# Multiplying the root of the norm in behind the products, in block 1 of a two-block transformer kernel

## What is computed

```python
def rmsnorm(x, g):
    y = xf * lax.rsqrt(jnp.mean(xf * xf, axis=-1, keepdims=True) + RMS_EPS)
    return (y * g).astype(x.dtype)

for l in range(2):
    h = rmsnorm(x, norm_mix_pre[l])
    a_in, b_x, b_b, b_c, q, k, v, gate_in = split_cols(h @ w_in[l], IN_SPLITS)
    ...                                             # pool, convolution, dilated attention, gates
    x = x + rmsnorm(merged @ w_out[l], norm_mix_post[l])
    h = rmsnorm(x, norm_mem_pre[l])
    x = x + rmsnorm(memory_cross_attention(h, mem_n, w_mq[l], w_mkv[l], w_mo[l]), norm_mem_post[l])
    h = rmsnorm(x, norm_ffn_pre[l])
    u = h @ w_up[l];  ua, ub = u[..., :D_FF], u[..., D_FF:]
    y = (jax.nn.silu(causal_dwconv(ua, conv_ffn_w[l])) * ub) @ w_down[l]
    x = x + rmsnorm(y, norm_ffn_post[l])
```

## Time and profile before

| | |
|---|---|
| median of 3 runs | 3808.35 us (3804.64 to 3812.05) |
| the profiled execution | 3807.09 us, span 3805.3 us |
| TensorE busy | 95% of the span |
| TensorE weight loads | 78% |
| VectorE busy | 53% |
| ScalarE busy | 40% |
| GpSimd busy | 6% |
| mean granted TensorE clock | 0.986 of full speed |

### The profile page before, as it was taken

One profiled execution on the slowest core, in us unless ns is written; L12 is line 12 of the kernel. 1 busy time (PEld: TensorE's weight loads), 2 busy tenths in 40 slices (PEclk: granted clock), 3 DMA queues, 4 the chain that ended last, 5 costly groups with the idle time before them and its releaser, 6 DMA issues.

```text
span 3805.3 us, 52598 instructions
## 1 busy us (share of the span) xinstructions
PE 3605.1 (95%) x19348; PEld 2957.6 (78%) x19348; DVE 2018.6 (53%) x3396; ACT 1504.8 (40%) x2302; POOL 241.7 (6%) x384
## 2 busy tenths in 40 slices
PE   8999989999999998899999988899999998899998
PEld 6788876887787887688778776788888777667886
DVE  4634466777764455577774465442333444644344
ACT  4344354332324534533235366432122334743233
POOL 0000000001000000000000052000000002610000
PEclk9999999999999999999999999999999999999999
DMA  3222322446332233144551102111211122112322
GB/s 132 93 72 95 98 80 83 147 140 195 119 99 78 71 106 108 42 149 139 191 164 56 50 2 42 45 50 61 66 61 61 55 63 58 31 45 78 99 94 83
DMA packets 113071, 333.14 MB, mean 88 GB/s; under 512 B 32792, under 2 KB 33688, under 8 KB 112408
## 3 DMA queue, kind: packets, MB, share of 16 engines
q1 hardware_dynamic: 74112, 265.23, 21.6%
q0 software_dynamic: 14400, 52.44, 4.3%
q10 hardware_dynamic: 24408, 13.46, 1.6%
HBM read 328.99 MB, written 6.00 MB: 88 GB/s over the span
## 4 chain that ended last, share of the span: by engine, by line
PE 82%; DVE 8%; ACT 6%; issue 2%; DVEq 1%; POOL 0%; ACTq 0%; DMA 0%; POOLq 0%; SPq 0%
PE PS L602 14%; PE PS L604 13%; PE PS L603 13%; PE PS L984 10%; PE PS L985 10%; PE PS L987 10%; PE PS L1112 1%; PE PS L677 1%; PE PS L771 1%; ACT PB L1675 1%; ACT FULL_P L1675 1%; ACT L1366 1%; PE PS L783 1%; DVE HVAL L1958 1%; DVE Y L2371 1%
## 5 line engine op out<-in xcount | busy, mean ns | idle before, releaser
L1914 DVE TENSOR_TENSOR WL<-RAW,WH 128x1024 fp32r<-128x1024 f32 x494 | 604.5, 1224 | 573.5 <-ACT WH L1330 568.2
L1330 ACT ACTIVATE WH<-RAW 128x1024 fp32r<-128x1024 f32 x494 | 521.2, 1055 | 636.3 <-PE PS L987 350.2
L602 PE MATMUL PS<-HHI,WH 128*128 128x512 f32 x1632 | 651.2, 399 | 24.5 <-DVE HLO L1951 16.2
L604 PE MATMUL PS<-HHI,WL 128*128 128x512 f32 x1632 | 639.9, 392 | 0.0
L603 PE MATMUL PS<-HLO,WH 128*128 128x512 f32 x1632 | 638.0, 391 | 0.0
L984 PE MATMUL PS<-H2HI,WH 128*128 128x512 f32 (+1 forms) x1336 | 470.0, 352 | 0.0
L985 PE MATMUL PS<-H2LO,WH 128*128 128x512 f32 (+1 forms) x1336 | 446.6, 351 | 0.0
L602 PEld LDWEIGHTS PS<-HHI,WH 128*128 128x128 f32 x1632 | 307.4, 188 | 105.3 <-issue 19.7
L987 PE MATMUL PS<-H2HI,WL 128*128 128x512 f32 (+1 forms) x1336 | 387.4, 350 | 0.0
L604 PEld LDWEIGHTS PS<-HHI,WL 128*128 128x128 f32 x1632 | 307.1, 188 | 70.5
L603 PEld LDWEIGHTS PS<-HLO,WH 128*128 128x128 f32 x1632 | 307.3, 188 | 64.3 <-issue 0.5
(11 more groups left out here) (353 smaller groups left out, 5737.0 us busy)
## 6 DMA issues: line engine op xcount, KB each, us to landing
RAW<-in_stream SPq DMA_DIRECT2D x494, 512.0 KB, 3.6
MODW<-in_modw POOLq DMA_DIRECT2D x96, 512.0 KB, 4.6
bias_rows<-in_rpb ACTq DMA_DIRECT2D x8, 476.2 KB, 6.7
X<-in_x SPq DMA_DIRECT2D x4, 512.0 KB, 5.5
MEM<-in_mem ACTq DMA_DIRECT2D x2, 1024.0 KB, 4.9
CROW<-in_crow POOLq DMA_DIRECT2D x4, 512.0 KB, 4.7
BIAS<-bias_rows ACTq DMA_DIRECT2D x8, 224.0 KB, 5.0
GRID<-bias_rows ACTq DMA_DIRECT2D x8, 224.0 KB, 4.6
```

What stands on the lines that cost most here:

```text
L602: nc.tensor.matmul(out, WH[:, slot, b * P:(b + 1) * P], hi, start=start, stop=False)
L604: return nc.tensor.matmul(out, WL[:, slot, b * P:(b + 1) * P], hi, start=False, stop=stop)
L1330: A(WH[:, d, :], RAW[:, s, :], ACT.Copy).then_inc(high_split, 1)
L1914: TT(WL[:, d, :], RAW[:, s, :], WH[:, d, :].bitcast(F32), ALU.subtract).then_inc(split_ready, 1)
```

## The change

At each of the six norms of x in block 1 (mix, memory and feed-forward in both layers), HHI and HLO are first written from X * gain without the root, right behind the residual (`raw_high`, `raw_low`), and two units run over them in `raw_pair`, the second two blocks behind the first. Where `sums` is set, a 128x512 matmul of the squares stands in front of each block of the first unit.

- Mix: units 0 and 1 run raw into banks 1 and 4 and get the root on VectorE in the pooling. The norm is then applied as before for the units from 2 on; their HVAL may only overwrite HLO when `raw_pair` has read it (`raw_read`), and the splits of units 2 and 3 stand inside `norm_apply`.
- Memory: all four query units run raw, and VectorE multiplies the root in where ScalarE copied before (`head_in`). `statistics` stands behind the raw pair.
- Feed-forward: all 44 units run raw. The root goes into RF, and GpSimd multiplies UA and later FC by it, in place, for each j. VectorE's order within a j is changed.

At the start the loads are reordered. The core of the diff:

```diff
@@ -466,11 +475,17 @@
 
             sp.dma_start(ONES[:], consts[:, P:2 * P]).then_inc(ones_in, 16)
             sp.dma_start(COL[:], consts[:, 2 * P:2 * P + 16]).then_inc(ones_in, 16)
+            sp.dma_start(PAR[:], params1).then_inc(par_in, 16)
 ...
+            def first_units(s0, s1):
+                for s in range(s0, s1):
+                    sp.dma_start(RAW[:, s, :], stream[s, :, :]).then_inc(landed[s], 16)
 ...
             for j in range(4):
                 sp.dma_start(X[:, 2 * j:2 * j + 2, :], x[:, 2 * j:2 * j + 2, :]).then_inc(x_part[j], 16)
-            sp.dma_start(PAR[:], params1).then_inc(par_in, 16)
-            for s in range(RAW_SLOTS):
-                sp.dma_start(RAW[:, s, :], stream[s, :, :]).then_inc(landed[s], 16)
+                if j == 1:
+                    first_units(0, SPLIT_AHEAD)
+            first_units(SPLIT_AHEAD, RAW_SLOTS)
 ...
-                for u in range(MOD_LAYER):
+
+                def load_modulation(u):
                     if u >= 2:
 
                         pool.wait_ge(mod_used, l * MOD_LAYER + u - 1)
                     pool.dma_start(MODW[u % 2][:], modw[l * MOD_LAYER + u, :, :]).then_inc(modw_in[u % 2], 16)
+
+                load_modulation(0)
+                load_modulation(1)
+                for j in range(FF):
+                    pool.wait_ge(taken[0], UP_TAKEN[l] + j + 1)
+                    nc.gpsimd.tensor_tensor(UA[:, 0, 8:8 + T], UA[:, 0, 8:8 + T], RF[:], ALU.mult).then_inc(up_scaled, 1)
+                    if j:
+                        load_modulation(j + 1)
+                    pool.wait_ge(silu_ready, l * FF + j + 1)
+                    nc.gpsimd.tensor_tensor(FC[:, 0, :], FC[:, 0, :], RF[:], ALU.mult).then_inc(gate_scaled, 1)
+                for u in range(FF + 1, MOD_LAYER):
+                    load_modulation(u)
 
             def keep_low(dst, src, hi, n):
 
@@ -612,19 +640,19 @@
                 last.then_inc(units_done, 1)
 ...
+            def raw_pair(hi, lo, sums, more, release=False, clock=18):
 
                 slots = [(m.n["units"] + x) % SLOTS for x in range(2)]
-                keep_clock(16)
-                pe.wait_ge(split_ready, m.at("units", 2))
+                keep_clock(clock)
                 for slot in slots:
                     set_in(slot)
+                for k in range(KB + RAW_LAG):
+                    if k < KB:
+                        if sums:
+                            m.add("sq")
+                            pe.wait_ge(sq_ready, m.at("sq"))
+                            nc.tensor.matmul(FLAT[:, 6 * T:7 * T], ONES[:], SQ_RAW[:, k % 3, :], start=k == 0, stop=k == KB - 1,
+                                             skip_group_check=True).then_inc(sq_summed, 1)
+                        if k == 0:
+                            pe.wait_ge(split_ready, m.at("units", 2))
+                        m.add("lo")
+                        pe.wait_ge(lo_ready, m.at("lo"))
+                        last = products(bank(3 * slots[0] + more), slots[0], k, hi[:, k, :], lo[:, k, :], k == 0, k == KB - 1)
+                        if k == KB - 1:
+                            unit_out(last)
+                    if k >= RAW_LAG:
+                        c = k - RAW_LAG
+                        last = products(bank(3 * slots[1] + more), slots[1], c, hi[:, c, :], lo[:, c, :], c == 0, c == KB - 1)
+                        if release and c < KB - 1:
+                            last.then_inc(raw_read, 1)
+                unit_out(last)
+
 ...
                 for k in range(KB + LAG):
+                    if behind and k in (0, LAG):
+                        pe.wait_ge(split_ready, m.at("units", 1 + (k == LAG)))
                     if k < KB:
 ...
             pe.wait_ge(ones_in, 32)
-            sum_squares(T, 0)
-            pe.wait_ge(consts_in, 16 * 5)
             for l in range(DEPTH):
 
-                chunk_pair(HHI, HLO)
+                raw_pair(HHI, HLO, True, 1, release=True, clock=18 if l else 0)
+                if l == 0:
+                    pe.wait_ge(consts_in, 16 * 5)
+                chunk_pair(HHI, HLO, behind=1)
                 if l == 0:
                     memory_sums()
-                with m.loop(pe, (C_V - 2) // 2, units=2, use0=1, use1=1):
+                with m.loop(pe, (C_V - 4) // 2, units=2, use0=1, use1=1):
                     chunk(HHI, HLO)
 ...
                 for _ in range(KB):
                     chunk(NHI, NLO, TC)
+
+                raw_pair(HHI, HLO, False, 1)
                 statistics(T)
-
-                chunk_pair(HHI, HLO)
                 for _ in range(HEADS - 2):
-                    chunk(HHI, HLO)
+                    chunk(HHI, HLO, behind=1)
                 sets_idle()
 ...
                 statistics(T)
-                sum_squares(T)
-
-                chunk_pair(HHI, HLO)
+
+                raw_pair(HHI, HLO, True, 0)
                 with m.loop(pe, FF - 1, units=2, use0=1, use1=1):
                     chunk(HHI, HLO)
                     chunk(HHI, HLO)
 ...
                                 unit_out(last)
                 statistics(T)
-                if l < DEPTH - 1:
-                    sum_squares(T)
 ...
+            def raw_high(k, gain):
+                A(HHI[:, k, :], X[:, k, :], ACT.Identity, scale=gain(k)).then_inc(hi_ready, 1)
+
+            def raw_and_squares(gain, arrived):
+
                 for k in range(KB):
+                    arrived(k)
+                    if k >= 3:
+                        act.wait_ge(sq_summed, m.at("sum", k - 2))
+                    A(SQ_RAW[:, k % 3, :], X[:, k, :], ACT.Square, scale=D ** -0.5).then_inc(sq_ready, 1)
+                    raw_high(k, gain)
+                m.add("sum", KB)
 ...
+            def unit_spent():
+                unit_wait()
+                split_high()
 ...
-            def of_x0(k, dst, n):
+            def x_landed(k):
+                if k == 4:
+                    for _ in range(SPLIT_AHEAD):
+                        split_high()
                 if k % 2 == 0:
                     act.wait_ge(x_part[k // 2], 16)
 ...
-            squares_summed(of_x0, T)
-            for _ in range(SPLIT_AHEAD):
-                split_high()
-            root(T, summed=True)
+            act.wait_ge(par_in, 16)
+            raw_and_squares(mix_gain(0), x_landed)
             m.add("mem", 16)
             for l in range(DEPTH):
 
+                root(T, summed=True)
                 act.wait_ge(layer_ready, l + 1)
                 act.dma_start(POOLW[:], poolw[l, :, :, :]).then_inc(pool_in, 16)
-                norm_high()
+                unit_spent()
+                norm_high((0, 1))
+                unit_spent()
+                norm_high(range(2, KB))
+                for c in range(2):
+                    p = (m.n["units"] - 2 + c) % SLOTS
+                    m.add(f"use{p}")
+                    A(U[:, c, :], bank(3 * p + 1), ACT.Copy).then_inc(taken[p], 1)
                 if l == 0:
                     memory_squares()
-                for c in range(2):
-                    take(U[:, c, :].unsqueeze(1))
                 if l == 0:
                     memory_root()
 ...
-                squares(of_x, T, before=lambda k: take(KV[:, k:k + 1, :], TC))
+                def of_x_raw(k, dst, n):
+                    of_x(k, dst, n)
+                    raw_high(k, lambda k: PL[:, G_MEM + k:G_MEM + k + 1])
+
+                squares(of_x_raw, T, before=lambda k: take(KV[:, k:k + 1, :], TC))
                 act.preload_act_table(ACT.Ln)
+                unit_spent()
+                unit_spent()
                 root(T)
-                norm_high()
-                for c in range(HEADS):
-                    take(QM[:, c:c + 1, :])
+                unit_spent()
+                unit_spent()
+                m.add("use0", HEADS // 2)
+                m.add("use1", HEADS // 2)
 ...
-                squares_summed(of_x, T)
                 act.preload_act_table(ACT.Ln)
-                root(T, summed=True)
-                norm_high()
 ...
+                raw_and_squares(lambda k: PL[:, G_FFN + k:G_FFN + k + 1], x_arrived)
+                root(T, dst=RF[:], summed=True)
 ...
+                def up_chunks(i, first=False):
                     for b in range(2):
                         take(UA[:, 0:1, 8:8 + T])
+                        if first and b == 0:
+                            condition()
                         m.add("conv")
 ...
+                up_chunks(0, first=True)
+                with m.loop(act, FF // 2 - 1, units=4, use0=2, use1=2, conv=2, **QUAD) as i:
+                    up_chunks(i)
 ...
-                    root(T, summed=True)
+                    raw_and_squares(mix_gain(l + 1), x_arrived)
 ...
+            def raw_low(k, gain):
+
+                m.add("hi")
+                dve.wait_ge(hi_ready, m.at("hi"))
+                STT(HLO[:, k, :], X[:, k, :], gain(k), HHI[:, k, :].bitcast(F32), ALU.mult, ALU.subtract).then_inc(lo_ready, 1)
+
```

(76 more changed lines are left out.)

69 lines of the change are left out of this document (42 added, 27 removed).

## The result

The changed kernel takes 3819.7 us in the median of 8 runs (3815.9 to 3823.0), the kernel before 3807.9 (8 runs, 3803.4 to 3813.8). The ratio is 1.0029, with a 95% interval of 1.0019 to 1.004: slower by 7 to 15 us, 11.8 in the medians. The forecast was 3816, 7.7 slower. In the profiled executions the span went from 3805.3 to 3817.0.

What follows compares the result with a forecast made beforehand. TensorE, busy 95% of the span, was taken as the bound. Start -14.0, layer 1's start -2.6, memory part +9.4 and feed-forward -0.5 sum to -7.7, 7.7 us slower: 3816 us, range 3800 to 3832.

Steps and rivals of the forecast that it cites:

- The start: Layer 0's start: memory sums, root, sines, tables and pooling now come behind units 2 and 3; loss 14.0 us, bounds 10 to 16.
- the root is hidden at the start: Rival: old start load-bound, or sine chain runs beside units 2 and 3; start costs 5 us, not 14; 3807; chance 0.10.
- Layer 1's start: Layer 1's mixing norm: WL of unit 4 waits behind norm_apply and pooling of chunk 0; loss 2.6 us, bounds 1.7 to 5.
- The memory part: Memory part of both layers: raw query units, root off the path; gain 4.7 us each, 9.4 in all, bounds 3 to 6 each.
- The front of the feed-forward part: Feed-forward part up to unit 3, both layers: unit 2 starts slow 3 us behind the raw pair; gain 2.8 us each.
- The loop's end: Last up turn to down products: TensorE waits longer for FLO, loss 3.05 us each layer, slow restart before and after alike.
- the clock holds: Rival: gaps of 2.4 to 4 us do not lower the granted clock, giving back 14.0 us; 3802; chance 0.17.
- The loop's period: Up products: GpSimd's multiplies fit into each turn, period stays 10.98 us, cost 0.
- the margin: Up loop: time from FT's end to its bank's reuse by the next unit; 1.4 us, or 0.8 if the engines exclude each other.
- the loop tips over: Rival: GpSimd's multiply over about 1.7 us instead of 1.27, or waiting, makes 42 turns late; 3829 to 3845; chance 0.14.
- its signs: If right: WL wait at 56 to 69 us, query copies near 534, turns of 10.98, FLO wait 6 to 7 us.

Runs made afterwards that it cites:

- 6: Changed kernel with one more GpSimd multiply (128x384, result unread) in each turn of the up products: 3841.52 us, ratio 1.0086 to the kernel before.
- 7: Changed kernel with two more GpSimd multiplies (128x384, results unread) in each turn of the up products: 3878.90 us, ratio 1.0181 to the kernel before.
- 5: Changed kernel with 24 unread matmuls behind the last up unit, in the gap before the down products: 3811.56 us, ratio 1.0011 to the kernel before.
- 12: Kernel before with 14 unread matmuls ahead of its down products and nothing else: 3806.23 us, ratio 0.9999 to the kernel before.
- 9: Changed kernel with the start's chain taken apart and 24 unread matmuls behind the last up unit: 3793.80 us, ratio 0.9969 to the kernel before.

## Right and wrong, step by step

**The sum was right in sign and 4 us short of the medians**, 2 short of its own terms measured over many executions. It is best compared with many profiled executions, since TensorE's restarts behind the same wait are slow in one and not in another. Means over all profiled executions with the same code in a stage:

| stage | old code | new code | difference | forecast |
|---|---|---|---|---|
| start | 477.9 (4 executions) | 493.4 (5; 491.8 to 494.6) | +15.5 | +14.0 |
| layer 1's start | 464.7 (3) | 466.9 (6; 466.3 to 467.6) | +2.2 | +2.6 |
| memory part, each | 120.9 (4) | 115.3 (24; 113.2 to 117.0) | -5.5 | -4.7 |
| root to A_1, each, without the multiplies added in 6 and 7 | 40.0 (10) | 36.3 (14; 35.5 to 38.3) | -3.7 | -2.8 |
| A_21 to the end of the layer, each, no unread matmuls | 137.6 (6) | 142.7 (6) | +5.1 | +3.05 |

15.5 + 2.2 - 11.1 - 7.3 + 10.2 = 9.5 (each stage of a layer twice); the medians differ by 11.8, and the interval reaches down to 7. That the sum came so close is in part luck: the start and the loop's end cost 1.5 and 4.1 more than forecast, and the other stages gave 3.8 more, so most of the error cancelled. The unchanged second block varies by itself between 1825.8 and 1829.7, which is the +1.4 of the first table's last row.

**The start**: right in mechanism, step for step. The last sum ended at 32.5 (31.0 forecast; the first product came at 15.30, where both WL were forecast for 14.1), the first product of unit 4 came 39.3 later (38.6), behind a wait of 13.4 (12). The bounds of 10 to 16 held the mean of 15.5, but not the profiled execution's 16.6. The rival that the root is hidden at the start, 0.10, was wrong.

**Layer 1's start**: right within the noise. The root of the residual came at 1009.13 and TensorE's last sum ended 22.4 behind the residual's start (22.8); unit 3 was copied at 1055.07, which is 12.75 later than before where the stage began 10.8 later.

**The memory part**: right, and a little better than said.

**The front of the feed-forward part**: the gain was underrated, because the forecast took unit 2's restart for slow. After a wait of 2.99 us it was slow in 4 of 14 cases (37.8 to 38.3 us for the stage) and not in 10 (35.5 to 35.9). In the changed kernel, layer 0, the product after it takes 0.50 us where the slow ones take 0.79:

```profile
639.96 0.50 PE L630 MATMUL PS<-HHI,WH 128*128 128x512 f32 x1 [2.99 <-DVE WL L2009]
```

**The loop's end is the step that failed.** "Its slow restart is there before and after": with the old order TensorE waits 3.5 us, and the restart was slow in 2 of 6 cases; with the new one it waits 6.55 us or more, and the restart was slow in 10 of 10. So to the 3.05 of order, which the waits bear out (3.0 and 3.1), came a slow restart, up to 2.8 us, that the old kernel mostly did not pay: 5.1 in the mean and not 3.05. Experiments 5 and 12 show both halves: unread matmuls give the new order 8 us in the medians and the old one nothing that can be told. The rival "the clock holds" treated each restart as slow in both kernels or in none; here the longer wait went with the slow one.

**The loop's period**: 10.98, cost 0, as forecast, but the margin named was the wrong one. The forecast followed FT to the reuse of its bank, 1.4, or 0.8 with exclusion. Experiments 6 and 7 leave about 0.5: VectorE's round closes earlier, with 0.99 us ahead of its first WL, and each shift makes new collisions with GpSimd. The rival "the loop tips over" asked for 1.7 us in place of 1.27 for a multiply. They took 1.31 and 1.55 in the mean, and experiment 6 shows that a delay of 0.9 is already too much. The forecast was nearer to that edge than it said. Of its signs, one did not come: VectorE's ops of two SBUF inputs were to be longer by about 1 us, and the two WL splits of a turn are longer by 0.25 and 0.5.

**What helped and what hurt, in one line**: against the kernel before, the memory part alone is worth 7.7 us; with everything changed, the start's chain apart and the clock held it is 13, and with the last turn in its own order 17.

## What to carry to other kernels

When work that waits for a root is moved behind products, list what else was queued behind the place where the engine used to stand, and move that too: here the products were right and the 16 us lay in a chain of sums, sines and tables that had been hidden beside them. The length of an engine's idle gap is a price of its own, beside the time itself: fill a long gap with products that nobody reads (here 6.6 us filled gave 8 us in the medians, 3.5 us filled gave nothing that could be told), and do not read from a single profile whether a restart behind a short one is slow. In a loop that two engines fill in turn, look for the idle time of each engine's own round, not for the slack of one result, before anything is added or reordered.

## What the runs showed of the hardware

- The same wait can be followed by a slow restart or not. At the down products: 0 of 10 restarts at the lower clock after idle gaps of 0.4 to 1.3 us (unread matmuls ahead), 1 of 2 after 2.5, 2 of 6 after 3.5, 10 of 10 after 6.55 to 9.1. A slow one ran its first three to five blocks at up to 1.44 us, mostly 1.28, instead of 0.69 and cost 1.6 to 2.9 us. The groups over 3 us differ in the order of the loop too, not in the wait alone; in the new order the wait alone was shortened, by unread matmuls, in experiments 5 and 9: 0 of 4.
- The length of the last gap is not all. At unit 2 of the up products 4 of 18 restarts were slow after 3.0 us. In experiments 6 and 7 waits for FT of 2.26, 2.01 and 3.25 us, 8 to 9 us behind such a gap, were each followed by slow blocks; in the second the first block still took 0.78 us and the third 1.28.
- A VectorE copy of 128x2 and the modulation op, started just behind a GpSimd multiply, last until its end or longer: 1.29 instead of 0.17 us and 2.33 instead of 1.21; GpSimd's multiply takes longer as well, 2.27 instead of 1.30 when it starts behind a WL.
- GpSimd's multiply of 128x512 takes 1.30 us undisturbed, in line with the 0.456 and 1.821 of the earlier trace rows (1.27 between them); 128x384 takes 0.90, 0.1 less than a straight line between the two gives.
